# First attention group: the products with the values of two blocks ago stand ahead of the next logits on TensorE

## The reference, cut to what matters

```python
q = rms_norm((rms_norm(x, g_norm) @ w_q).reshape(b, s, 16, 64), g_q).reshape(b, nb, 128, 4, 4, 64)
logits = einsum("bntkgd,bnskd->bnkgts", q, k_band) * 64 ** -0.5        # own block and the one before
logits = where(in_window & ~first_blk, logits + bias, -inf)
m = maximum(max(logits, -1), sink)
p = exp(logits - m);  denom = sum(p, -1) + exp(sink - m);  p = p / denom
o = einsum("bnkgts,bnskd->bntkgd", p, v_band)
return o.reshape(b, s, 1024) @ w_o
```

## Time and profile before

| | |
|---|---|
| median of three runs | 1911.54 us |
| profiled execution: whole time / span | 1912.03 / 1910.3 us |
| busy over the span: PE / DVE / ACT / POOL | 1880.3 / 1460.4 / 909.0 / 491.6 us |
| mean granted TensorE clock | 0.999 |
| chain that ended last, share of PE | 88% |
| first attention group on PE, q_transpose of block 1 to step_out(7) | 1054.04 to 1090.67 us |

### The profile page before, as it was taken

One profiled execution on the slowest core, in us unless ns is written; L12 is line 12 of the kernel. 1 busy time (PEld: TensorE's weight loads), 2 busy tenths in 40 slices (PEclk: granted clock), 3 DMA queues, 4 the chain that ended last, 5 costly groups with the idle time before them and its releaser, 6 DMA issues.

```text
span 1910.3 us, 25899 instructions
## 1 busy us (share of the span) xinstructions
PE 1880.3 (98%) x8776; PEld 1563.4 (82%) x8776; DVE 1460.4 (76%) x2150; ACT 909.0 (48%) x1591; POOL 491.6 (26%) x428
## 2 busy tenths in 40 slices
PE   8999999999999999999999899999999999999999
PEld 7888888788888888888988787878788888888887
DVE  5476768988788876787854688899978887877875
ACT  6243435544444444444522777756444444444443
POOL 0000001424242410011120677751433333301010
PEclk9999999999999999999999999999999999999999
DMA  4111332122222249963111010040212221279681
GB/s 181 45 56 38 105 133 89 67 99 83 82 73 92 86 145 311 288 148 63 42 58 33 1 56 23 12 155 34 100 66 88 88 88 66 99 259 306 179 165 67
DMA packets 63106, 198.95 MB, mean 104 GB/s; under 512 B 5168, under 2 KB 5296, under 8 KB 55856
## 3 DMA queue, kind: packets, MB, share of 16 engines
q1 hardware_dynamic: 48368, 163.29, 24.0%
q0 software_dynamic: 14656, 34.61, 8.4%
HBM read 162.22 MB, written 35.65 MB: 104 GB/s over the span
## 4 chain that ended last, share of the span: by engine, by line
PE 88%; DVE 6%; ACT 2%; issue 2%; DMA 1%; POOL 1%; ACTq 0%; SPq 0%; DVEq 0%
PE banks L2450 28%; PE banks L2452 28%; PE banks L2451 28%; DVE xT L1956 1%; PE banks L2850 1%; DVE xT L1963 1%; DMA b<-c_scratch 1%; DVE fw_lo L1914 1%; PE banks L2836 1%; PE banks L2837 1%; PE banks L2609 1%; PE banks L2823 0%; PE banks L2872 0%; ACT p_later L1489 0%; DVE xT L1972 0%
## 5 line engine op out<-in xcount | busy, mean ns | idle before, releaser
L2450 PE MATMUL banks<-t_hi,fw_hi 128*128 128x512 f32 x1248 | 487.5, 391 | 5.1 <-DVE xT L1923 1.3
L2452 PE MATMUL banks<-t_hi,fw_lo 128*128 128x512 f32 x1248 | 485.8, 389 | 0.0
L2451 PE MATMUL banks<-t_lo,fw_hi 128*128 128x512 f32 x1216 | 473.3, 389 | 0.0
L2450 PEld LDWEIGHTS banks<-t_hi,fw_hi 128*128 128x128 f32 x1248 | 234.3, 188 | 58.2 <-issue 2.5
L2452 PEld LDWEIGHTS banks<-t_hi,fw_lo 128*128 128x128 f32 x1248 | 234.3, 188 | 49.1
L2451 PEld LDWEIGHTS banks<-t_lo,fw_hi 128*128 128x128 f32 x1216 | 228.3, 188 | 47.0
L770 POOL TENSOR_TENSOR nrm<-raw 128x512 f32<-128x512 f32 x40 | 55.7, 1392 | 710.9 <-DVE fw_lo L1914 430.8
L2450 PE MATMUL banks<-fw_hi,fw_hi 128*128 128x512 f32 x544 | 211.9, 389 | 1.9 <-DVE fw_lo L2073 1.9
L2452 PE MATMUL banks<-fw_hi,fw_lo 128*128 128x512 f32 x544 | 211.7, 389 | 0.0
L2451 PE MATMUL banks<-fw_lo,fw_hi 128*128 128x512 f32 x544 | 211.7, 389 | 0.0
L1318 ACT ACTIVATE fw_hi<-b 128x512 fp32r<-128x512 f32 x154 | 97.0, 631 | 228.0 <-PE banks L2452 215.2
(11 more groups left out here) (252 smaller groups left out, 3783.1 us busy)
## 6 DMA issues: line engine op xcount, KB each, us to landing
raw<-in_w_f_in SPq DMA_DIRECT2D x44, 1024.0 KB, 4.8
c_scratch<-xT SPq DMA_DIRECT2D x44, 512.0 KB, 2.6
b<-c_scratch SPq DMA_DIRECT2D x16, 1024.0 KB, 9.6
a_sum<-in_w_f_out POOLq DMA_DIRECT2D x16, 1024.0 KB, 14.5
raw<-in_w_f_out SPq DMA_DIRECT2D x54, 256.0 KB, 10.4
w_raw<-in_w_ao SPq DMA_DIRECT2D x16, 512.0 KB, 3.5
x_scratch<-xT SPq DMA_DIRECT2D x4, 2048.0 KB, 7.7
xT<-x_scratch SPq DMA_DIRECT2D x8, 1024.0 KB, 17.4
```

What stands on the lines that cost most here:

```text
L2450: nc.tensor.matmul(out, w_h, m_h, start=start, stop=False, **kw)
L2451: nc.tensor.matmul(out, w_h, m_l, start=False, stop=False, **kw)
L2452: return nc.tensor.matmul(out, w_l, m_h, start=False, stop=stop, **kw)
```

## The change

In the first group (`j == 0`) the call of `weighted(block - 2)` moves from behind `p_transpose(block - 1)` to ahead of `logits(n + 1, 2)`, in the blocks n = 2 to 6. In the last block of the group (`last`, n = 7) and in the other three groups it stays where it was.

```diff
@@ -2913,13 +2913,15 @@
                     if last and more:
                         pe.wait_ge(lg_done, blk.now(1))
                         keys_transpose()
+                    if j == 0 and block >= 2 and not last:
+                        weighted(block - 2)
                     if j == 0 and not last:
                         logits(n + 1, 2)
                     if block:
                         p_transpose(block - 1)
                     if j and not last:
                         logits(n + 1, 2)
-                    if block >= 2:
+                    if j and block >= 2 or last:
                         weighted(block - 2)
                     if last and more:
                         pe.wait_ge(kT_ready, grp.now())
```

## The result

The changed kernel took 1919.36 us (median of 7 runs, 1917.62 to 1919.70), the kernel before 1911.54 us (7 runs, 1911.00 to 1913.97). The ratio is 1.0035, 95% interval 1.0024 to 1.0046. A second set of runs of the changed kernel, beside other kernels, gave 1.0038 [1.0024, 1.0051]. So the change costs 6.7 to 7.3 us, with an interval of 4.6 to 9.7 over both. The profiled execution took 1919.7 us, its span is 1918.0 us.

The account below looks back on a forecast made before the run. PE is busy 98% of the span, but in the first group the wait chain through POOL to `step_out(7)` bounds it. Delay 4.8 us plus clock 1.4 makes 6.2 us: median 1917.7 us, 8-in-10 range 1914.0 to 1921.5.

Parts of the forecast that it names:

- PE's gaps for `qT` and the late `o_sum`: Blocks 4 to 6: moved products cannot fill PE's 2.2 us of gaps, as `o_sum` comes late; rival that they do, 0.06.
- Block 2, 0.54 us: In block 2 `weighted(0)` waits for nothing and delays logits 3 by its own length, 0.54 us.
- The ring: From block 3 logits wait for `weighted`, which waits for DVE's `o_sum` behind earlier logits: 5.66 us per round, 6.80 in blocks 3, 4.
- The price of 1.14 us: DVE's time between the reductions and `pT_lo`, for the weight split in block 3 and the values in block 4: 1.14 us each.
- `step_out(7)` 4.8 us late at full clock: First PE work behind the moved products that the chain of waits reaches; starts about 1095.5 instead of 1090.67, 4.8 us later.
- What would show it: Signs in the changed trace: PE's longest waits for `o_sum`, no `qT` waits, later logits, `step_out(7)` near 1095.5 to 1097.5, clock 0.5 somewhere.
- Nothing returned behind the group: After `step_out(7)` the whole 4.8 us delay stays to the end; rival that half is returned, 1913.9 us, chance 0.10.
- The slower stretch cost nothing before: In the kernel before, 1.2 GHz from 1086.4 to 1089.8 cost nothing, because POOL's chain ran beside it.
- The clock, 1.4 us taken: PE's longer idle time likely drops the clock to 1.2 GHz before `weighted(2)` or `weighted(3)`; 1.4 us taken, forecast range 0 to 2.5.
- My upper bound, 1.8 + 2.1 = 3.9 us: Clock cost if `weighted(2)` with logits 5 and `weighted(3)` with logits 6 and a set of transposes all run slow: 3.9 us.
- the clock stays low through blocks 4 to 6: Rival: 1.2 GHz lasts through blocks 4 to 6, adding 4.8 + 3.9 us for 1920.2 us; chance 0.12.
- Ready operands: In blocks 4 to 6, products whose operands stood ready would run in PE's `qT` waits and save 2.2 us, giving 1909.3 us.

Follow-up runs that it names:

- changed kernel with fillers: Changed kernel plus 512-column matmuls whose result nobody reads, ahead of the moved value products in blocks 3 to 6; ratio 1.0027 against the kernel before.
- products of three blocks ago: Kernel before, but value products of three blocks ago stand ahead of the logits in blocks 4 to 7 of the first group; ratio 1.0058.
- with `qT` first: Kernel before, value products of three blocks ago ahead of the logits in blocks 4 to 6, ACT copying `qT` ahead of `o_small`; ratio 1.0015.
- the sums first: Changed kernel, but DVE makes `pT_lo` and `o_sum` ahead of the weight split in block 3 and the values in block 4; ratio 1.0025 against before.
- `o_lo` first: Kernel before, but POOL makes `o_lo` of block 3 ahead of scaling the probabilities of block 6 in the first group; ratio 0.9997.

## Why the prediction was right, and which term was off

- **PE's gaps for `qT` and the late `o_sum`**: right. The rows ahead of the change showed `o_sum` at 1078.18 for logits that started at 1076.15, and that was enough to reject the filling of gaps.
- **Block 2, 0.54 us**: `weighted(0)` took 0.47 us (1067.43 to 1067.90).
- **The ring, 6.80 and 5.66 us from logits to logits**: 1067.90 to 1074.71 is 6.81. At full clock (changed kernel with fillers) the next ones are 1076.04 to 1082.86, 6.82, and 1082.86 to 1088.56, 5.70. The price of 1.14 us, taken for the split of the weight and for the values, is confirmed by their removal (1.12 and 1.14).
- **`step_out(7)` 4.8 us late at full clock**: 4.64 measured with fillers.
- **What would show it**: PE's waits ahead of `weighted(1)` to `(4)` were forecast at about 1, 4, 3 and 3 us and came as 0.96, 3.83, 2.69 and 1.86. `step_out(7)` was to start between 1095.5 and 1097.5; it started at 1098.89, outside, by the clock. POOL's `o_lo` still releases it, but only its last three pieces, from 1096.21 on, stand back to back, and ahead of them POOL waits 1.71 us for ACT.
- **Nothing returned behind the group**: from `step_out(7)` to the first logits of group 1 it is 6.41 us before and 6.40 after, and from there to the end the difference of 0.5 us is within the scatter of 2.9 us between traces.
- **The slower stretch cost nothing before**: shown, 26.78 against 26.79 us.
- **The clock, 1.4 us taken**: this term was mis-sized. It measured 3.34 and 4.26 us. The step that failed is "I take 1.4 us: a stretch of 3.4 us". I counted one such stretch; there were 10.2 us at 1.2 GHz in one execution and 13.7 us in the other. In rows: `weighted(2)` to the transposes of p behind logits 5 took 3.25 us (1080.52 to 1083.77) against 1.96 with fillers, 1.3 us more; `weighted(3)` and logits 6 took 3.55 us against 1.95, 1.6 more, and the slow transposes behind them about 0.45 more. My upper bound, 1.8 + 2.1 = 3.9 us, was close to what came, and the rival "the clock stays low through blocks 4 to 6" with its 1920.2 us lies nearer the measured 1919.4 us than the forecast of 1917.7. As a mechanism it is not what happened: the clock came back after 3.4 us, between the two sets of products, and fell again ahead of the second. I had argued against it from the one stretch that ended by itself before. There PE had work all through it (3.40 of 3.40 us busy in the earlier trace rows); in the ring it was idle again for 2.69 us before the next products.
- **Ready operands**: the prediction took it that products with ready operands would fill PE's gaps and save 2.2 us. The runs with products of three blocks ago show +3.24 us at full clock, and about +1.8 with `qT` first: ACT's `o_small` waits for them. The sum did not use this.

The terms 4.64 + 3.34 = 7.98 us are those of one execution. The medians give 7.8 us and the ratio 6.7 us, with an interval from 4.6 to 8.8, which is too wide to split a whole time into ring and clock. The ways split it: where the clock is the same they repeat to 0.1 us (26.79 and 26.78; to `weighted(2)` 16.40 and 16.39 in the two executions of the changed kernel), and what the clock adds differs between executions by about 1 us.

## What to carry to other kernels

Before work is pulled ahead in an in-order stream to fill a gap, write down who makes its operands and whether that engine is itself waiting for what now stands behind the work. If so the two engines take turns, and the length of a round is the sum of both, block after block. A wait inside such a round is paid each time. What a single one costs depends on where it stands: logits that came 1.65, 3.3 and 2.8 us late lengthened the way by 1.66, 2.64 and 0.12 us. Where the wait leaves TensorE idle, the work behind it may run at 1.2 GHz and must be priced so.

## What the runs showed of the hardware

- After the wait of 3.83 us ahead of `weighted(2)` the granted clock was 0.50 in both executions of the changed kernel. After waits of 2.7 us it was either: 0.50 ahead of `weighted(3)` in both, but with the sums first still 1.00 after the first wait of 2.70 us and 0.50 after the second (a first product of 0.47 and then of 0.77 us in the rows). With fillers of 512 columns in the waits it stayed 1.00 over the whole way.
- Whether it falls at small waits differs between executions: the kernel before with the waits of the earlier trace rows had a stretch at 0.50 from 1086.4 us on, and the one with `o_lo` first, which has the same three waits, 2.2 us in total, had none in this group. The two kernels differ only from POOL's work at 1088.7 us on, behind that fall, so that the difference is not the edit's.
- At 1.2 GHz four value products and eight logits matmuls took 3.55 us (1087.50 to 1091.05), at 2.4 GHz 1.95 us (1087.56 to 1089.51, with fillers), a factor of 1.82.
